# Recurrent block, turn from head to head: ten small instructions from VectorE to ScalarE, query products first

## What is computed

```
for each chunk of 64 tokens, for each head:
    b     = cumsum(g)                                   # g = log of the forget gate
    att   = sum_k q[t,k] * k[s,k] * exp(b[t,k] - b[s,k])   for s <= t
    o     = att @ v + (q * exp(b)) @ state
    state = exp(b_last) * state + (k * exp(b_last - b))^T @ v
```

## Time and profile before

| | us |
|---|---|
| three timed runs | 3333.97, 3334.14, 3340.61 |
| their median | 3334.14 |
| the profiled execution, its own time | 3338.97 |
| its span, first to last instruction | 3337.5 |
| TensorE busy in the span | 3083.0 (92%) |
| VectorE busy | 1850.7 (55%) |
| ScalarE busy | 961.7 (29%) |
| GpSimd busy | 1910.0 (57%) |
| mean granted TensorE clock | 0.965 |

### The profile page before, as it was taken

The page is one execution under the profiler, slowest core; times in us unless marked ns, Lnnn a source line. Parts: engine busy times, 40 slices in busy tenths (PEclk is TensorE's granted clock), DMA queues, the critical chain, the costliest instruction groups (busy, mean ns, idle before and its releaser), DMA issues.

```text
span 3337.5 us, 39578 instructions
## 1 busy us (share of the span) xinstructions
PE 3083.0 (92%) x15146; PEld 2396.7 (72%) x15146; DVE 1850.7 (55%) x2681; ACT 961.7 (29%) x1563; POOL 1910.0 (57%) x1860
## 2 busy tenths in 40 slices
PE   8899989989999999998998999997889998898997
PEld 5687767768778877776876777776677776686675
DVE  6754876741384478676128433335788888512313
ACT  5334213430223421344012323233433333301102
POOL 5565656547676655655667555554556555375451
PEclk9899999999999999999999999999999999999997
DMA  5232222133222222122422222221112121222221
GB/s 195 83 106 103 78 74 76 64 108 137 102 101 102 95 83 88 63 76 89 142 100 96 79 78 79 78 74 60 64 64 76 64 76 64 97 103 88 71 94 59
DMA packets 61069, 294.55 MB, mean 88 GB/s; under 512 B 5680, under 2 KB 10672, under 8 KB 31440
## 3 DMA queue, kind: packets, MB, share of 16 engines
q1 hardware_dynamic: 36384, 247.48, 21.2%
q10 hardware_dynamic: 24496, 44.54, 3.9%
HBM read 274.10 MB, written 16.84 MB: 87 GB/s over the span
## 4 chain that ended last, share of the span: by engine, by line
PE 62%; DVE 27%; ACT 5%; issue 2%; POOL 2%; DMA 1%; DVEq 0%; ACTq 0%; POOLq 0%
PE bank L396 53%; DVE bank L1942 5%; DVE h_lo L1681 2%; DVE rec_cum L2240 1%; DVE rec_ex L2283 1%; POOL w_lo L2464 1%; DVE rec_small L2269 1%; PE bank L735 1%; PE bank L752 1%; PE bank L744 1%; PE bank L924 1%; DVE last_z L2412 1%; DVE bank L1752 1%; POOL w_hi L2462 1%; DVE newton L1660 1%
## 5 line engine op out<-in xcount | busy, mean ns | idle before, releaser
L396 PE MATMUL bank<-h_hi,w_lo 128*128 128x512 f32 x3712 | 1523.2, 410 | 86.9 <-DVE h_lo L1681 32.8
L396 PE MATMUL bank<-h_hi,w_hi 128*128 128x512 f32 x3712 | 1468.8, 396 | 0.0
L396 PE MATMUL bank<-h_lo,w_hi 128*128 128x512 f32 x3712 | 1467.8, 395 | 0.0
L2462 POOL TENSOR_SCALAR w_hi<-w_raw 128x512 fp32r<-128x512 f32 x928 | 673.5, 726 | 1288.7 <-PE bank L396 1224.4
L2464 POOL TENSOR_TENSOR w_lo<-w_raw,w_hi 128x512 fp32r<-128x512 f32 x928 | 1259.6, 1357 | 77.4
L396 PEld LDWEIGHTS bank<-h_hi,w_lo 128*128 128x128 f32 x3712 | 711.2, 192 | 313.5 <-issue 54.6
L396 PEld LDWEIGHTS bank<-h_hi,w_hi 128*128 128x128 f32 x3712 | 709.7, 191 | 155.1
L396 PEld LDWEIGHTS bank<-h_lo,w_hi 128*128 128x128 f32 x3712 | 711.6, 192 | 151.4 <-issue 12.5
L965 ACT ACTIVATE raw<-bank 128x512 f32<-128x512 f32 x148 | 88.6, 598 | 390.3 <-PE bank L396 362.4
L1942 DVE SCALAR_TENSOR_TENSOR bank<-cfm_up,par,bank 128x512 f32<-128x512 f32 x232 | 175.4, 756 | 8.3
L2100 DVE TENSOR_TENSOR xT<-bank,xT 128x512 f32<-128x512 f32 x32 | 22.1, 692 | 221.7 <-PE bank L396 221.0
(11 more groups left out here) (336 smaller groups left out, 2876.7 us busy)
## 6 DMA issues: line engine op xcount, KB each, us to landing
w_raw<-in_wall SPq DMA_DIRECT2D x230, 1024.0 KB, 4.9
x_scratch<-xT ACTq DMA_DIRECT2D x12, 1024.0 KB, 4.7
xT<-x_scratch ACTq DMA_DIRECT2D x12, 1024.0 KB, 6.8
ssd_abc<-acs_scratch ACTq DMA_DIRECT2D x16, 512.0 KB, 3.7
first_xin<-in_x SPq DMA_DIRECT2D x4, 1024.0 KB, 11.6
out<-last_rows ACTq DMA_DIRECT2D x4, 1024.0 KB, 4.3
w_raw<-in_wall SPq DMA_DIRECT2D x8, 256.0 KB, 10.6
raw<-in_wpp ACTq DMA_DIRECT2D x16, 128.0 KB, 2.5
```

Source lines behind the costliest of these rows:

```text
L396: mm = t.matmul(bank[BANK[u]][:, :], w[:, CS16[k]], h[:, k, :], start=(k == 0 and w is m.w_lo[b]), stop=(k == KT - 1 and w is m.w_hi[b] an ...
L2462: g.tensor_scalar(m.w_hi[b][:, part], m.w_raw[b][:, part], 1.0, 1.0, ALU.mult, ALU.mult).then_inc(*s.hi.inc(u, n))
```

## The change

- VectorE's `gather` (four copies, L2320) is gone. ScalarE has a new step `near(j)` with the same four copies, after its exponentials of far(j+1); it waits for VectorE's sum into `near` (new event `near`). combine(j) waits for ScalarE's event `near` in place of `am`.
- VectorE's six scalings in `far` (L2269) are gone. ScalarE has a new step `far_small(j)`, behind near(j-1) in its order, with the same six as ACTIVATE Copy with a per-partition scale. It waits for a new event `fq`, the two query products.
- VectorE's four products of far now come in the order lq0, lq1, lk0, lk1; the last two carry the event `fk`. far(j) on TensorE waits for `fk` and for ScalarE's `q2`.
- ScalarE's gates(j) waits for `fk` in place of `q2`. blocks(j) on VectorE waits for ScalarE's near(j-1).

```diff
@@ TensorE @@
         def far(j):
-            t.wait_ge(*dve.at("q2", j))
+            t.wait_ge(*dve.at("fk", j))
+            t.wait_ge(*act.at("q2", j))
         def combine(j):
-            t.wait_ge(*dve.at("am", j))
+            t.wait_ge(*act.at("near", j))
@@ ScalarE @@
         def gates(j):
-                a.wait_ge(*dve.at("q2", j - 1))
+                a.wait_ge(*dve.at("fk", j - 1))
+        def near(j):
+            a.wait_ge(*dve.at("near", j))
+            for x in range(0, P, 32):
+                a.wait_ge(*act.now())
+                a.activation(q.diag[x:x + 32, :, x:x + 32], q.near[x:x + 32, :].rearrange("p (c n) -> p c n", n=32),
+                             ACT.Copy).then_inc(*act.inc("near", j))
+        def far_small(j):
+            Q = lambda d, c: q.lq[d][:, CS[c]]
+            w = [q.g2[:, d, c:c + 1] for d in range(2) for c in range(2)]
+            a.wait_ge(*dve.at("fq", j))
+            for n, (src, f1) in enumerate(((Q(0, 2), w[0]), (Q(0, 3), w[1]), (q.small[:, 1, :], w[0]), (Q(1, 0), w[2]),
+                                           (Q(1, 1), w[3]), (q.small[:, 3, :], w[3]))):
+                a.wait_ge(*act.now())
+                a.activation(q.small[:, n, :], src, ACT.Copy, scale=f1).then_inc(*act.inc("q2", j))
         logs(0)
         far(0)
+        far_small(0)
         decays(0, 0)
...
             gather(j)
             far(j + 1)
+            near(j)
+            far_small(j + 1)
             decays(j + 1, 0)
...
         gather(7)
+        near(7)
         output(7)
@@ VectorE @@
         def far(j):
-            for dst, x, y, name in ((q.lq[0], q.ex[1][:, 0, :], q.qs[:, :], "far0"), (q.lk[0], q.gx[:, 1, :], kd[:, 0, :], "far1"),
-                                    (q.lq[1], q.gx[:, 0, :], q.qs[:, :], "far2"), (q.lk[1], q.ex[1][:, 1, :], kd[:, 1, :], "far3")):
+            for dst, x, y, name, done in ((q.lq[0], q.ex[1][:, 0, :], q.qs[:, :], "far0", "fq"),
+                                          (q.lq[1], q.gx[:, 0, :], q.qs[:, :], "far2", "fq"),
+                                          (q.lk[0], q.gx[:, 1, :], kd[:, 0, :], "far1", "fk"),
+                                          (q.lk[1], q.ex[1][:, 1, :], kd[:, 1, :], "far3", "fk")):
                 v.wait_ge(*act.at(name, j))
                 v.wait_ge(*dve.now())
-                v.tensor_tensor(dst[:, :], x, y, ALU.mult).then_inc(*dve.inc())
-            v.wait_ge(*act.at("far4", j))
-            for n, (src, f1) in enumerate(((Q(0, 2), w[0]), (Q(0, 3), w[1]), (None, w[0]), (Q(1, 0), w[2]), (Q(1, 1), w[3]),
-                                           (None, w[3]))):
...
-                v.tensor_scalar(q.small[:, n, :], src, f1, None, ALU.mult).then_inc(*dve.inc("q2", j))
+                v.tensor_tensor(dst[:, :], x, y, ALU.mult).then_inc(*dve.inc(done, j))
         def blocks(j):
+            if j:
+                v.wait_ge(*act.at("near", j - 1))
...
-        def gather(j):
-            v.wait_ge(*act.at("am", j))
-            for x in range(0, P, 32):
-                v.tensor_copy(q.diag[x:x + 32, :, x:x + 32], q.near[x:x + 32, :].rearrange("p (c n) -> p c n", n=32)
-                              ).then_inc(*dve.inc("am", j))
```

More of the change, by code:

```diff
@@ L2253, in far @@
             kd = q.kd[j % 2]
-            for dst, x, y, name in ((q.lq[0], q.ex[1][:, 0, :], q.qs[:, :], "far0"), (q.lk[0], q.gx[:, 1, :], kd[:, 0, :], "far1"),
-                                    (q.lq[1], q.gx[:, 0, :], q.qs[:, :], "far2"), (q.lk[1], q.ex[1][:, 1, :], kd[:, 1, :], "far3")):
+            for dst, x, y, name, done in ((q.lq[0], q.ex[1][:, 0, :], q.qs[:, :], "far0", "fq"),
+                                          (q.lq[1], q.gx[:, 0, :], q.qs[:, :], "far2", "fq"),
+                                          (q.lk[0], q.gx[:, 1, :], kd[:, 0, :], "far1", "fk"),
+                                          (q.lk[1], q.ex[1][:, 1, :], kd[:, 1, :], "far3", "fk")):
                 v.wait_ge(*act.at(name, j))
                 v.wait_ge(*dve.now())
-                v.tensor_tensor(dst[:, :], x, y, ALU.mult).then_inc(*dve.inc())
-            Q = lambda d, c: q.lq[d][:, CS[c]]
-            w = [q.g2[:, d, c:c + 1] for d in range(2) for c in range(2)]
-            v.wait_ge(*act.at("far4", j))
-            v.wait_ge(*dve.now())
-            for n, (src, f1) in enumerate(((Q(0, 2), w[0]), (Q(0, 3), w[1]), (None, w[0]), (Q(1, 0), w[2]), (Q(1, 1), w[3]),
-                                           (None, w[3]))):
-                if src is None:
-                    v.wait_ge(*dve.now())
-                    src = q.small[:, 1 if n == 2 else 3, :]
-                v.wait_ge(*dve.now())
-                v.tensor_scalar(q.small[:, n, :], src, f1, None, ALU.mult).then_inc(*dve.inc("q2", j))
+                v.tensor_tensor(dst[:, :], x, y, ALU.mult).then_inc(*dve.inc(done, j))
         def decays(j, n):
@@ L2313, in blocks @@
             v.wait_ge(*dve.now())
-            v.tensor_reduce(q.near[:, :], q.small[:, :, :].rearrange("p l x -> p x l"), AX.X, ALU.add).then_inc(*dve.inc())
-        def gather(j):
-            v.wait_ge(*act.at("am", j))
-            for x in range(0, P, 32):
-                v.wait_ge(*dve.now())
-                v.tensor_copy(q.diag[x:x + 32, :, x:x + 32], q.near[x:x + 32, :].rearrange("p (c n) -> p c n", n=32)
-                              ).then_inc(*dve.inc("am", j))
+            v.tensor_reduce(q.near[:, :], q.small[:, :, :].rearrange("p l x -> p x l"), AX.X, ALU.add).then_inc(*dve.inc("near", j))
         def mean(j):
@@ L2361, in recurrent @@
             blocks(j)
-            gather(j)
             query(j + 1)
@@ L2379, in recurrent @@
         blocks(7)
-        gather(7)
         gate(6)
```

## The result

The changed kernel took 3314.37 us (median of four runs, 3312.16 to 3319.02); the kernel before, run beside it, 3336.23 us (3333.97 to 3340.61). The ratio is 0.9935, 95% interval 0.9918 to 0.9952: faster by 0.65%, some 22 us, where the sum had said 29.9. The time lies inside the range of 3290 to 3322. The profiled execution took 3319.02 us with a span of 3317.6.

The account below looks back on a forecast made before the run. VectorE was taken to bound the turn between heads, making TensorE, the spine, wait. Terms 3.0 + 2.0 + 10.8 + 5.1 + 3.5 + 5.5 = 29.9 us, off the median 3334.14, gave 3304 us; range 3290 to 3322.

Parts of the forecast that it names:

- Before head 0: Far of head 0 starts 2.6 us earlier and its matmuls shed some slow clock: 3.0 us gained.
- Turn 0 to 1: Combine starts 1.8 us earlier, far's 0.91 wait goes, minus 0.7 for the lowered clock: 2.0 us gained.
- Odd turns: Turns 1 to 2, 3 to 4, 5 to 6: far's whole 3.59 us wait goes, 10.8 us; clock afterwards, 5.1.
- the clock's 5.1 us: Behind the three odd-turn waits, slow-clock work of 3.4 us takes 1.7 at the full level: 5.1 us gained.
- Even turns: No gain at far; level 0 waits shrink, with the clock: 3.5 us in head 5, 5.5 in head 7.
- L820's 30.0 us: TensorE's waits at levels 2 to 6, said mostly to move with TensorE: gain 0.
- The signs: Expected row evidence: no far waits in turns 1 to 7, head 7's level 0 near 1.7 us, L815 waits no longer.
- Rival 1: At levels 0 and 1 VectorE, slowed by GpSimd, isn't ready; 14 us of gain remain, 3320 us; chance 0.17.
- Rival 2: VectorE's head start spares a levels 2 to 6 wait in three or four heads: 12 us more, 3292; chance 0.12.
- Rival 3: ScalarE is the slower place, its copies and scalings in series delaying far: 3345 us; chance 0.04.

Follow-up runs that it names:

- the reordered kernels: Changed kernel with VectorE's gates(j+1) moved behind level 6: 3300.37 us; also with ScalarE's level 4 exponential ahead of an evacuation: 3295.07 us.
- the doubled kernel: Changed kernel with each of ScalarE's ten small instructions (copies and scalings) issued twice, same result: 3322.14 us, 0.9949.

## Why the prediction was right, and where it was wrong

**Before head 0: 3.0 predicted.** The wait went from 6.84 to 3.91, 2.9 us. Right; the scalings ended with the keys, and the row's releaser is now the key product.

**Turn 0 to 1: 2.0 predicted.** The wait at combine went from 9.08 to 7.19, the 0.91 at far is gone, and combine's eight matmuls took 5.83 us for 5.27: 1.9 + 0.9 - 0.6 = 2.2. Right at the turn, with the loss under the lowered clock. But from far of head 0 to far of head 1 only 1.2 us were gained (65.3 to 64.1): the rest was lost in head 0's levels, ahead of combine.

**Odd turns: 10.8 + 5.1 predicted.** The three waits at far are gone, and no new one stands in their place in the turn. But the clock's 5.1 us can't be told apart in the result, because the same three heads now stand still at level 6. The 4 us behind that wait, head 1 of the changed kernel:

```profile
2406.20:2410.20 4.00, 3.44 (x44) 2.79 (x41) 3.28 (x4) 3.75 (x6) 3.84 (x3) 0.57 0.02 4
```

The lowered clock that used to follow the wait at far follows this one instead. Over the whole block the mean granted clock rose from 0.93 to 0.95.

**Even turns: head 5, 3.5; head 7, 5.5.** Head 5's 1.80 became 1.21, and head 3 has the same (before: 0.50). Head 7 is the step that failed. I had written that its wait "ends on products that may not start before far's matmuls are done", and so would shrink to those products' 1.66 us. It grew to 6.60, since VectorE wasn't there. VectorE's timeline in that turn:

```profile
2794.07 3.18 DVE L2295 TENSOR_TENSOR rec_ex<-rec_cum 128x256 f32<-128x256 f32 x4
2797.36 0.91 DVE L1679 TENSOR_TENSOR newton<-rec_th 128x512 f32<-128x512 f32 x1
2798.30 1.65 DVE L1681 SCALAR_TENSOR_TENSOR newton<-newton,rec_th 128x512 f32<-128x512 f32 x1
2799.98 0.99 DVE L1683 SCALAR_TENSOR_TENSOR rec_th<-newton,rec_th 128x512 f32<-128x512 f32 x1
2801.09 1.55 DVE L2338 SCALAR_TENSOR_TENSOR xT<-xT,par,rec_th 128x512 f32<-128x512 f32 x1
2802.67 3.03 DVE L2295 TENSOR_TENSOR rec_ex<-rec_cum 128x256 f32<-128x256 f32 x4
2805.84 0.69 DVE L2309 TENSOR_TENSOR rec_lq<-rec_ex,rec_qs 128x512 f32<-128x512 f32 x1
```

Far started at 2798.07 and was done by about 2801, and the products began at 2805.84 with no idle row in between: differences, the norm's end, differences again, each longer than undisturbed since GpSimd was splitting from 2784 to 2804. I had taken the releaser of the products from the buffers and not added up the queue in front of them. The prediction's own numbers spoke against it: in the kernel before too the products started at 2828.55, 4.5 us after far was done (2824.05). This place came out 7.5 us below the sum (5.5 gained against 2.0 lost). The wait is 4.9 of it (6.6 for 1.7), the clock behind it 1.0, and 1.6 was lost between level 0 and the last combine (36.5 us became 38.1), which the sum didn't cost at all. Against the profiled pair the sum was 10.0 us too high: these 7.5 and the 4.0 of scatter ahead of the block and behind it, less 1.5 that the block up to head 7 gained beyond it. The kernel with the norm's end moved confirms the cause of the wait, though it found the next wait close behind.

**L820's 30.0 us: 0 predicted.** The total rose by 3.4. The reason given, that these waits "move with TensorE", holds for the 1.8 us at level 4 in each head. It misses the 2.8 us at level 6, where VectorE's wait for the sigmoid, TensorE's earlier arrival and GpSimd's splitting meet; the reordered kernels remove them. I had looked at where TensorE waits in heads 1 and 2 at the turn, not at level 6, and so didn't see that the two exclude each other. The time came out near the sum for the block up to head 7 only since three heads lost that wait while three others gained it. From far to far, the sum's terms put 14.3 us into heads 1, 3 and 5 (10.8 and 3.5) and 5.1 into heads 2, 4 and 6; measured were 4.1 and 17.6. That the totals are near each other, 19.4 and 21.8, is luck. With the copies alone all six heads have the wait, and half the gain is gone.

**The signs.** Far waits nowhere in turns 1 to 7, combine of head 0 starts 1.4 us after the sum into `near`, the wait before head 0 is 3.9, and ScalarE's scalings take 0.40 us: as written. Head 7's level 0 didn't, and level 0 and 1 wait 13.0 us in all for 12.1. The levels' waits grew by 4.3 us (L816 and L821), well under half of the 16.5 that the turns lost.

**The rivals.** Rival 1, given back in the levels (3320), holds in part: head 7 and 1.21 us in two heads. Its reason, VectorE slowed by GpSimd, was the right one. Its sum was off: half of 15.9 and two thirds of 9.0 are 14 us given back, which leaves 16 of the 29.9 and gives 3318. Rival 2, a wait in the levels spared in some heads, happened in heads 2, 4 and 6, with its opposite in 1, 3 and 5. Rival 3 is refuted: ScalarE's prices are 0.40 and 0.31 us as taken, and even doubled they cost only 5 us. As for what the Trainium skill says, "ScalarE: Activation LUTs", section "Rules for kernel authors", to multiply on VectorE: with the splitting cut short VectorE is indeed quicker (286 ns against 403). Beside GpSimd's work it isn't (749), and the measurement decides: 22 us faster, not slower. With this agrees what the Trainium skill, "SBUF — State Buffer", section "Who interferes with whom", says of ScalarE's own ports: its 403 ns were the same with the full splitting and with the cut.

**What stays open.** The rows show that heads alternate with the clock behind level 4, not what decides between 0.57 and 1.00 there, after waits of the same 1.8 us. So it isn't shown either why the roles swapped with the change, why all six heads are of one kind with the copies alone, or why the scalings alone and the doubled kernel show yet other patterns. Each pattern is read from one execution, so it isn't shown that it is the same in all executions of a kernel. A kernel with the 13 us of slower differences removed alone wasn't tried, nor one with only the products' new order.

## What to carry to other kernels

Price a small instruction by its rows beside the engine that disturbs it, not by its mean: here moving ten of them a head to ScalarE paid 22 us, and some 4 once GpSimd's splitting was cut short. When waits alternate between repeats of a loop, look for a second wait that hides the first in every other repeat; removing either alone uncovers the other, and both can be worth more than the sum (43 us here, for 13 and 22). Before saying that a wait shrinks to what its releaser needs, add up everything in the releasing engine's queue from its last idle row on.

## What the runs showed of the hardware

Plain two-input instructions of VectorE in float32 lengthen beside GpSimd's splitting: the same product of 128x512 took mostly 0.69, 0.91 or 1.60 us, with a few between, and 0.69 on average in all of far's products with the splitting cut short. GpSimd's own instructions were drawn out too. GpSimd's timeline of the changed kernel, turn 6 to 7:

```profile
2786.75 1.29 POOL L2469 TENSOR_TENSOR w_lo<-w_raw,w_hi 128x512 fp32r<-128x512 f32 x1
...
2789.16 1.60 POOL L2469 TENSOR_TENSOR w_lo<-w_raw,w_hi 128x512 fp32r<-128x512 f32 x1
```

In the same turn VectorE's four far products took 0.91, 1.60, 0.92 and 1.60 us. I had expected the effect for the copies and scalings, less for products of two tensors. ScalarE's 128x128 scaling kept 0.40 us throughout.
